# Output products of two layers end one token tile after the other, with norm and first feed-forward chunks in the same order

## The reference

```python
mixed = retention_mixer(normed, ...)   # or nsa_mixer; both end in  o @ w_out
h = h + rms_norm_2(mixed, mix_norm_post[layer])
normed = rms_norm_2(h, ffn_norm_pre[layer])
h = h + rms_norm_2(swiglu_ffn(normed, ...), ffn_norm_post[layer])

def swiglu_ffn(x, w_in, w_out):        # 2816 hidden columns
    gate, up = jnp.split(x @ w_in, 2, axis=-1)
    return (jax.nn.silu(gate) * up) @ w_out
```

## Time and profile before

| | |
|---|---|
| median of 3 runs | 1240.26 us (1240.23 to 1240.45) |
| the profiled execution's own time | 1241.84 us |
| its span, first to last instruction | 1239.8 us |
| mean granted TensorE clock | 0.982 |
| busy: TensorE, VectorE, ScalarE, GpSimd | 1188.2, 764.5, 594.2, 179.5 us |

### The profile page before, as it was taken

The page is one execution under the profiler, slowest core; times in us unless marked ns, Lnnn a source line. Parts: engine busy times, 40 slices in busy tenths (PEclk is TensorE's granted clock), DMA queues, the critical chain, the costliest instruction groups (busy, mean ns, idle before and its releaser), DMA issues.

```text
span 1239.8 us, 19123 instructions
## 1 busy us (share of the span) xinstructions
PE 1188.2 (96%) x7392; PEld 1050.7 (85%) x7392; DVE 764.5 (62%) x1030; ACT 594.2 (48%) x826; POOL 179.5 (14%) x179
## 2 busy tenths in 40 slices
PE   7999999997999999999999799999799987999997
PEld 6999999996888887888878688888799876888885
DVE  6676544475887545555545677754776856777642
ACT  5666554334344344534344444443576755444431
POOL 1000000060223001211100122210101101222200
PEclk9999999998999999999999899999899998999999
DMA  9555335444455553654536355555443334555530
GB/s 354 181 192 188 127 112 204 169 146 160 170 183 193 217 198 133 221 197 142 175 131 237 121 201 178 194 204 183 146 172 120 103 123 151 201 174 198 175 131 34
DMA packets 31973, 212.04 MB, mean 171 GB/s; under 512 B 4169, under 2 KB 4829, under 8 KB 7592
## 3 DMA queue, kind: packets, MB, share of 16 engines
q1 hardware_dynamic: 28936, 201.68, 45.7%
q0 software_dynamic: 2688, 9.26, 2.0%
q10 hardware_dynamic: 288, 0.23, 0.1%
HBM read 210.08 MB, written 1.08 MB: 170 GB/s over the span
## 4 chain that ended last, share of the span: by engine, by line
PE 86%; issue 5%; DVE 3%; ACT 3%; POOL 2%; DMA 1%; SPq 0%; DVEq 0%; POOLq 0%; ACTq 0%
PE acc L431 41%; PE acc L518 18%; PE acc L520 9%; PE aux L431 9%; PE acc L471 1%; POOL gate L728 1%; PE acc L473 1%; PE acc L475 1%; PE aux L2299 1%; PE aux L2360 1%; ACT wh L404 1%; PE aux L1990 1%; PE aux L580 1%; DVE x L1695 1%; PE aux L2009 1%
## 5 line engine op out<-in xcount | busy, mean ns | idle before, releaser
L404 ACT ACTIVATE wh<-raw 128x2048 fp32r<-128x2048 f32 x190 | 364.0, 1918 | 278.8 <-PE acc L431 126.0
L412 DVE TENSOR_TENSOR wl<-raw,wh 128x2048 fp32r<-128x2048 f32 x126 | 288.3, 2294 | 274.3 <-ACT wh L404 266.5
L518 PE MATMUL acc<-hx,wh 128*128 128x512 f32 x960 | 338.6, 398 | 0.8 <-DVE hx L1573 0.8
L520 PE MATMUL acc<-hx,wl 128*128 128x256 f32 x960 | 269.4, 281 | 0.0
L431 PE MATMUL acc<-hx,wh 128*128 128x256 f32 x1280 | 234.3, 285 | 1.5 <-DVE hx L595 1.5
L518 PEld LDWEIGHTS acc<-hx,wh 128*128 128x128 f32 x960 | 181.7, 189 | 44.7 <-issue 1.9
L431 PEld LDWEIGHTS acc<-hx,wh 128*128 128x128 f32 x1280 | 200.5, 193 | 3.2 <-DVE wl L412 1.9
L419 DVE TENSOR_TENSOR wl<-raw,wh 128x1024 fp32r<-128x1024 f32 x128 | 164.4, 1284 | 37.4 <-ACT wh L404 37.4
L520 PEld LDWEIGHTS acc<-hx,wl 128*128 128x128 f32 x960 | 182.5, 190 | 0.0
L431 PE MATMUL acc<-hx,wl 128*128 128x256 f32 x640 | 181.5, 284 | 0.0
L431 PEld LDWEIGHTS acc<-hx,wl 128*128 128x128 f32 x640 | 123.2, 193 | 0.0
(11 more groups left out here) (350 smaller groups left out, 1843.9 us busy)
## 6 DMA issues: line engine op xcount, KB each, us to landing
raw<-in_stream SPq DMA_DIRECT2D x190, 1024.0 KB, 4.8
bias_b<-in_bias POOLq DMA_DIRECT2D x6, 512.0 KB, 5.2
grow<-in_grows POOLq DMA_DIRECT2D x4, 512.0 KB, 3.9
nbias<-strip POOLq DMA_DIRECT2D x4, 512.0 KB, 4.7
x<-in_x SPq DMA_DIRECT2D x2, 512.0 KB, 4.1
y<-x SPq DMA_DIRECT2D x1, 1024.0 KB, 3.9
s<-cums POOLq DMA_DIRECT2D x1, 512.0 KB, 4.4
decay<-in_decay POOLq DMA_DIRECT2D x1, 512.0 KB, 3.9
```

What stands on the lines that cost most here:

```text
L404: nc.scalar.activation(wh[:, s, :], raw[:, s, :], ACT.Copy).then_inc(hi_ready, 1)
L412: nc.vector.tensor_tensor(wl[:, s, :], raw[:, s, :], wh[:, s, :].bitcast(F32), ALU.subtract).then_inc(lo_ready, 1)
L518: nc.tensor.matmul(out[:, :], wh[:, s, cols], hx[:, k].rearrange("p a n -> p (a n)"), start=(k == 0), stop=False, skip_group_check=True)
L520: last = nc.tensor.matmul(out[:, 0:SEQ], wl[:, s, cols], hh[:, k, :], start=False, stop=(k == KT - 1), skip_group_check=True)
```

## The change

**TensorE.** The last two chunks of each output product's second column group are taken for tile 0 both, then for tile 1 both. Then `tile_pe` turns tile 0, the first two feed-forward chunks are used for tile 0, `tile_pe` turns tile 1, and the two chunks are used for tile 1. These two chunks go through `product_n` (tokens on partitions, 48 matmuls of 256 columns for a chunk), so their hidden values come out with tokens on partitions. The other 20 chunks go through `product_s` as before. The two chunks that are made first hold the last two of the 22 hidden tiles. After the first chunk of `ffn_out`, `late_turn` turns their values with four transposes.

**The other engines.** `post` and the norm are written for one tile at a time (`tile_mix`, `tile_x`, `tile_xn`, `tile_square`, `tile_x_square`, and `tile_post` on three engines). `x` is written and squared in two halves for each tile. The copies into `hx` are made for each tile. The split of the third feed-forward chunk, which ScalarE and VectorE made before the joint's `post`, stands inside the joint now. ScalarE's `silu_n` reads the `acc` bank of a late chunk directly, VectorE's `late` multiplies it and frees the bank. GpSimd's load of `grow2` stands behind both tiles' powers, where it stood ahead of the norm's.

```diff
+LATE = 2
+FFN_LOOP = FFN_KT - LATE
...
+            def tile_post(m):
+                for t in range(TT):
+                    pool.wait_ge(mean_in, TT * m + t + 1)
+                    g.tensor_tensor(rstd[:, t:t + 1], psum1[:, t:t + 1], mhalf[:, 0:1], ALU.pow).then_inc(mean_pow, 1)
+                    pool.wait_ge(x_sq, 4 * m + 2 * t + 2)
+                    g.tensor_scalar(means[:, t:t + 1], sums[:, 2 * t:2 * t + 1], sums[:, 2 * t + 1:2 * t + 2], EPS, ALU.add, ALU.add
+                                    ).then_inc(rstd_step, 1)
+                    rstd_steps[0] += 1
+                    pool.wait_ge(rstd_step, rstd_steps[0])
+                    g.tensor_tensor(stat[:, t, 7:8], means[:, t:t + 1], mhalf[:, 0:1], ALU.pow).then_inc(rr_out, 1)
...
+            tile_post(0)
             pool.wait_ge(post_done, TT)
             load(grow2[:], io["grows"][2:3, :].broadcast_to([P, D]), grow_in[2])
-            norm_pool(pool, 2)
             ffn_pool(0)
             post(1)
-            norm_pool(pool, 3)
...
+            def tile_square(n, name, cg, t, junk):
+                wait(act, post_sq, 4 * n + 2 * cg + t)
+                wide_unit(act, name, cg, t)
+                a.activation(junk[:, t, :], wide_bank(GROUP[name], cg, t), ACT.Square, scale=D ** -0.5,
+                             accum_out=psums[:, t, cg:cg + 1]).then_inc(post_sq, 1)
+            def tile_x_square(m, n, t):
+                for half in range(2):
+                    cols = slice(half * WW, (half + 1) * WW)
+                    act.wait_ge(*((post_done, TT * n + t + 1) if half else (x_half, TT * m + t + 1)))
+                    a.activation(xn[:, t, cols], x[:, t, cols], ACT.Square, scale=D ** -0.5,
+                                 accum_out=sums[:, 2 * t + half:2 * t + half + 1]).then_inc(x_sq, 1)
+            def tile_post(m, n, name, slot, junk, ahead):
+                tile_square(n, name, 1, 0, junk)
+                tile_x_square(m, n, 0)
+                tile_act(act, m + 1, m + 1, 0, range(0, 2), slot, hh)
+                tile_square(n, name, 1, 1, junk)
+                tile_act(act, m + 1, m + 1, 0, range(2, 8), slot, hh)
+                split_hi(act, ahead)
+                tile_x_square(m, n, 1)
+                tile_act(act, m + 1, m + 1, 1, range(0, 8), slot, hh)
...
+                def silu_n(i):
+                    act.wait_ge(mm_done, START[name] + i + 1)
+                    bank = acc[(GROUP[name] + i) % 2][:].rearrange("p (t n) -> p t n", t=TT)
+                    a.activation(fsil_n[:, i], bank[:, :, 0:P], ACT.Silu).then_inc(late_sil, 1)
+                split_hi(act, c0 + 1)
+                silu_n(0)
+                split_hi(act, c0 + 2)
+                silu_n(1)
...
+            def tile_mix(n, name, cg, t, mixed, grow):
+                cols = slice(cg * WW, (cg + 1) * WW)
+                dve.wait_ge(post_sq, 4 * n + 2 * cg + t + 1)
+                if cg:
+                    v.tensor_reduce(psum1[:, t:t + 1], psums[:, t, :], AX_X, ALU.add).then_inc(mean_in, 1)
+                v.tensor_tensor(mixed[:, t, cols], wide_bank(GROUP[name], cg, t), grow[:, cols], ALU.mult
+                                ).then_inc(acc_out[(GROUP[name] + t) % 2], 1)
+            def tile_x(m, n, name, t, mixed):
+                group_out(dve, GROUP[name] + 2 + t)
+                dve.wait_ge(mean_pow, TT * m + t + 1)
+                for half in range(2):
+                    cols = slice(half * WW, (half + 1) * WW)
+                    v.scalar_tensor_tensor(x[:, t, cols], mixed[:, t, cols], rstd[:, t:t + 1], x[:, t, cols], ALU.mult,
+                                           ALU.add).then_inc(post_done if half else x_half, 1)
+            def tile_xn(m, t):
+                dve.wait_ge(rr_out, TT * m + t + 1)
+                v.tensor_scalar(xn[:, t, :], x[:, t, :], stat[:, t, 7:8], None, ALU.mult).then_inc(xn_out, 1)
+            def tile_post(m, n, name, slot, mixed, grow, ahead):
+                tile_mix(n, name, 1, 0, mixed, grow)
+                tile_x(m, n, name, 0, mixed)
+                tile_xn(m, 0)
+                tile_dve(dve, m + 1, 0, range(0, 4), slot, hl, hh)
+                tile_mix(n, name, 1, 1, mixed, grow)
+                tile_dve(dve, m + 1, 0, range(4, 8), slot, hl, hh)
+                tile_x(m, n, name, 1, mixed)
+                split_lo_half(dve, ahead, 0)
+                tile_xn(m, 1)
+                split_lo_half(dve, ahead, 1)
+                tile_dve(dve, m + 1, 1, range(0, 8), slot, hl, hh)
...
+                def late(i):
+                    dve.wait_ge(late_sil, LATE * layer + i + 1)
+                    bank = acc[(GROUP[name] + i) % 2]
+                    v.tensor_tensor(ft_n[:, i], fsil_n[:, i], bank[:].rearrange("p (t n) -> p t n", t=TT)[:, :, P:CW], ALU.mult
+                                    ).then_inc(acc_out[(GROUP[name] + i) % 2], 1)
+                late(0)
+                split_lo(dve, c0 + 1)
+                late(1)
+                split_lo(dve, c0 + 2)
+                with dve.Fori(0, FFN_LOOP // 4) as it:
...
+            for t in range(TT):
+                ret_out(2, 1, (t,))
+                ret_out(3, 1, (t,))
...
+            def ffn_pe(layer):
+                i0, g0, m = START[f"ffn_in_{layer}"], GROUP[f"ffn_in_{layer}"], layer + 1
+                for t in range(TT):
+                    tile_pe(pe, m, m, t)
+                    for i in range(LATE):
+                        product_n(pe, i0 + i, g0 + i, hh, hl, ready=tiled(m, t), toks=(t,))
+                with pe.Fori(0, FFN_LOOP // 4) as it:
                     for s in range(4):
-                        product_s(pe, At(i0 + s, 4, it), At(g0 + 2 * s, 8, it), None if s else normed(before))
...
+            def late_turn(layer):
+                for i in range(LATE):
+                    group_out(pe, GROUP[f"ffn_in_{layer}"] + i)
+                    for t in range(TT):
+                        tr = nc.tensor.transpose(aux[:, 0, i * SEQ + t * P:i * SEQ + (t + 1) * P], ft_n[:, i, t, :], ident[:])
+                tr.then_inc(late_turned, 1)
+            ffn_pe(0)
```

More of the change, by code:

```diff
@@ L107, in nsa_work_banks @@
 def nsa_work_banks():
-    uses, freed = {}, [("norm_lo", 28 + 2 * KT)] * 4
+    uses, freed = {}, [("norm_lo", 20 + 2 * KT)] * 4
     n = 0
@@ L157 @@
 RET_AT = [dict(v=0, q=2, k=3, g=4)] + [dict(q=0, k=1, v=2, g=4)] * 3
+POST_AT = {1: 0, 3: 1}
 NORMS = ["mix", "mlp", "ret", "ffn0", "nsa", "ffn1"]
@@ L467, in product_n @@
                     k = k0 + kk
-                    if ready and t == 0:
+                    if ready and (t == 0 or toks == (1,)):
                         pe.wait_ge(*ready(k))
@@ L1134, in _ @@
+            for cg in range(2):
+                for i in range(4 - cg):
+                    split_hi(act, START["ret_out"] + 4 * cg + i + 3)
+                for t in range(TT if cg == 0 else 0):
+                    tile_square(0, "ret_out", 0, t, ry)
+            tile_post(0, 0, "ret_out", 3, ry, START["ffn_in_0"] + LATE)
             ffn_act(0)
@@ new lines, in ffn_dve @@
+                v.tensor_tensor(hid(hid2l), aux[:, 0, :], hid(hid2h).bitcast(F32), ALU.subtract).then_inc(late_lo, 1)
+            dve.wait_ge(setup, 2)
+            dve.wait_ge(grow_in[1], 16)
+            for cg in range(2):
+                for i in range(4 - cg):
+                    split_lo(dve, START["ret_out"] + 4 * cg + i + 3)
+                for t in range(TT if cg == 0 else 0):
+                    tile_mix(0, "ret_out", 0, t, mixed0, grow0)
+            tile_post(0, 0, "ret_out", 3, mixed0, grow0, START["ffn_in_0"] + LATE)
@@ L2543, in ffn @@
         res = [k_tiles(np.concatenate([win[:, P * j:P * (j + 1)], win[:, FFN + P * j:FFN + P * (j + 1)]], axis=1), 0)
-               for j in range(FFN_KT)]
+               for j in list(range(FFN_LOOP, FFN_KT)) + list(range(FFN_LOOP))]
         res += [k_tiles(wout, 0, WKT * i, WKT, WW) for i in range(5)]
```

147 lines of the change are left out of this document (74 added, 73 removed).

## The result

The changed kernel takes 1230.72 us, the median of 4 runs (1229.58 to 1231.21); the kernel before took 1240.24 us beside it (4 runs, 1239.79 to 1240.45). The ratio is 0.9914, with a 95% interval of 0.9897 to 0.9932: faster by 9.5 us, where 11.2 were forecast. The profiled execution took 1229.58 us with a span of 1227.5, against 1241.84 and 1239.8 before, so the two profiles stand 12.3 us apart.

What follows compares the result with a forecast made beforehand. TensorE was taken to bound the kernel, with time to win in its waits at two joints. Gains of 6.11 and 6.05 less 1.0 for `late_turn` made 11.2 us, from 1240.26 to 1229.1; range 1226.3 to 1232.8.

Steps and rivals of the forecast that it cites:

- Rival F: At the joints, the chain only moves: tile 1's `xn` comes some 6 us after tile 0's matmuls; near 1240, chance 0.03.
- Parts 3 and 5: Inside tile 0's first late chunk, TensorE waits 0.55 us for low part 3 and 0.51 for low part 5.
- What is late next: Early in the loop, late values free `acc` banks; the third claim is tight, 0.25 us idle at the second joint only.
- The rest: Outside the joints, `late_turn` loses 0.5 us per layer, 1.0 in all; chunk order and moved loads cost nothing.
- rival E: The third chunk's slot is loaded late and TensorE waits at each joint; slower, 1243 or so, chance 0.02.
- B: At the joints, the chain is slower than its rows as engines alternate between tiles and splits; 1231 to 1233, chance 0.16.
- C: TensorE's clock falls in the pieced joint; 1237 if 10 us at 1.2 GHz, about 1232.5 if 3 to 5; chance 0.10.
- D: Loop pace changes with code place: second layer at 5.55 gives 1227.0, chance 0.08; first at 5.65 gives 1231, chance 0.05.
- rival A: Both joints and the rest as summed, within a few tenths per piece; 1227.5 to 1230.7, chance 0.56.

Runs made afterwards that it cites:

- the kernel with the square moved: Changed kernel with tile 1's square, sum and `mixed` put ahead of tile 0's copies and low parts instead of in their middle; 1225.59 us, ratio 0.9886 to the kernel before.
- the output product whole: Changed kernel with the output products' last two chunks again done for both tiles at once; 1237.41 us, ratio 0.9968 to the kernel before.
- the late value delayed: Changed kernel with a needless ScalarE copy ahead of the first layer's first `silu_n`; 1231.38 us, ratio 0.9916 to the kernel before.
- the tuned joint: Changed kernel with tile 1's square first, whole splits moved behind tile 1's work, tile 1's transposes before the last six matmuls of tile 0's second chunk; 1226.46 us, ratio 0.9877.

## Why the prediction was right

**The mechanism.** The claim was a chain of latencies that work for the other tile can cover. It is shown from both sides: with half of the output matmuls behind tile 0's last one the wait grows from 0.33 to 3.06 us, and without tile 0's chunks from 0.25 to 7.54. Rival F, a chain that only moves, is what the kernel with both tiles turned first does, and not what the change does.

**The pieces.** From the output product's end, the forecast 0.67 + 8.35 + 0.54 + 7.29 = 16.85 reads 0.49 + 8.23 + 0.41 + 7.40 = 16.53:
- Before tile 0's transposes: 0.49 for 0.67. `x` starts 2.09 us after tile 0's last output matmul (676.91 to 679.00) for 2.20, since the power took 0.56 us where the earlier trace rows have 0.70, and `xn` starts 1.08 after the squares end (681.18 to 682.26) for 1.19.
- From tile 0's transposes to the end of its chunks (683.07 to 691.18 + 0.12): 8.23 for 8.35. Parts 3 and 5 are late by 0.34 - 0.12 = 0.22 and 0.49 - 0.12 = 0.37, for 0.55 and 0.51, together 0.47 less. Against that, from the transposes to the first matmul it took 1.63 for 1.55, and the first matmul after each of the three waits takes 0.20 to 0.22 instead of 0.12, which I had left out: 0.35 more. The two errors nearly cancel, and that is luck. That the waits stand at parts 3 and 5 was right, and the kernel with the square moved takes them away.
- Before tile 1's transposes: 0.41 for 0.54.
- From there to the loop: 7.40 for 7.29. Transposes to matmul took 1.54 for 1.55, and the matmuls 5.86 for 5.74.

**What is late next.** The third bank was claimed late at the second joint alone, and it cost 0.19 us for 0.25. The Silu table load of 1.28 us does it. The first joint has none, and its bank is freed 4.97 us after the loop's start (704.08), at the second 5.68 after it (1052.75). With both tiles turned first the load lies in ScalarE's idle time at the second joint (it ends at 1052.34, `silu_n` starts at 1057.90), and the bank is freed 4.97 after the loop's start again, with no wait. That 0.19 is near the forecast is luck: the bank is free only 0.03 us after TensorE was due at 1052.72, where the sum had 0.25; the rest is that the matmul starts 0.09 late and its successor 0.09 later still. The Trainium skill (ScalarE: Activation LUTs, section What ACT_TABLE_LOAD costs) gives 2.66 us for a switch of table with the drain. The trace of the changed kernel does not agree: the load starts as the split ends, and `silu_n` follows at 1045.44, 1.29 after the load's start. By that figure, as an estimate, the wait would be 1.4 us longer.

**The rest.** `late_turn` costs 0.48 and 0.41 us, forecast 0.5 each. The third chunk's slot (rival E) never held anything up: among TensorE's waits the only one for a DMA is one for `hot`, 7.6 us, far from here, and ScalarE's splits wait for a transfer four times, all in the first 28 us of the kernel.

**The rivals.** B (a slower chain) did not come: every wait is under its sum but the one ahead of tile 0's first matmul, which is 0.08 over. C (the clock) is wrong for this kernel: the windows read 1.00 with six idle pieces in 16.5 us. Of the windows over the joints that are shown here, those below 1.00 each hold a gap of 3 us or more: 0.63 before the change, 0.72 and 0.91 with the output product whole and 0.79 with both tiles turned. The Trainium skill (TensorE: Matmul & The Clock Gate, section A second HAM failure mode) speaks of a clock that falls through frequent short idle times; no run here shows it. D took place in both directions at once: the first loop took the pace of 5.65 and the second that of 5.55, so the sum of the loops came out as forecast. That is luck: the sum had 5.55 in the first and 5.65 in the second. And its cause as I put it, the place of the code, fell with the second profile of the kernel before.

**The size.** Profile against profile the change gives 12.3 us, of which the prediction's terms are 11.9 (12.81 less 0.89) against its 11.2; the gain of the joints was under-sized by 0.31 and 0.34 us. The medians give 9.5, and 10.5 in the repeat (1241.27 against 1230.8). The median of 1230.72 lies 1.6 above the forecast and at the upper edge of rival A. So by the medians the forecast gain of 11.2 is 1.7 and 0.7 too high, by the profiles 1.1 too low. What of this is the choice of chip and execution I can't say: the difference of 2 to 3 us between medians and profiles is inside the spread of one kernel's executions and no run located it.

**What stays open.** What sets the pace of a loop. Within a loop the pace is steady to about 0.02 us a chunk. In the changed kernel and its variants it follows a pattern: entered straight from `product_n`, the first loop ran at 5.65 in 7 of 7 profiles; with one transpose ahead, at 5.65; with two, at 5.55 in 3 of 3. The second loop starts at 5.65 and goes over to 5.55 right behind its bank wait of 0.2 us, in all but two: with the late value delayed it had the wait and stayed, and with both tiles turned first it had no wait and stayed. Against a pace that the code alone decides speaks, beside the kernel before, the feed-forward loop of the first block: it is the same and is entered in the same way in all 14 profiles, and ran at 5.55 in 12 and at 5.65 in two, those of the output product whole and of the tuned joint. So some chance is in it, and three profiles with two transposes are a strong hint and no proof. What is different inside the engine I don't know, and no run measured it.

## What to carry to other kernels

A norm between two products costs its chain of latencies only if no product of the other tile is left to run: cut the last chunks of the product before and the first of the product after by tile, and interleave both. Parts of it bring little or do harm (here a ratio of 1.0019 with the first cut alone, 0.9968 with the second alone, 1.0035 with both cuts but all transposes first, against 0.9914). When it is in, look at the order in the helpers' queues: what serves the other tile went better ahead of a row of copies than into its middle. An order change also changes when slots are freed, so look at what now gets ahead in the queue.

## What the hardware showed that I had not expected

One and the same loop of 512- and 256-column matmuls has two steady paces, 0.347 and 0.353 us for a pair, 5.55 and 5.65 for 16, at a granted clock of 1.00 in both. The loop keeps a pace for a hundred microseconds. Two dead transposes ahead of it went with the faster one in 3 of 3 profiles, one transpose did not; a bank wait of 0.2 us was followed by a switch in 10 profiles of 11, and an untouched loop elsewhere changed its pace between profiles. In 20 chunks that is 2 us, 0.16% of this kernel, for no change of work. So a difference of 1 to 2 us between two versions is not to be believed before the paces of their loops have been compared.
